# Fewer rows in the small experts' gathers and scatters, and another row order for the down weights and the activation

## The reference

```
gu = xb @ w_gate_up[e] + b_gate_up[e]          # 1024 -> 2048, rows xb = tokens of expert e
gate, up = jnp.split(gu, 2, axis=-1)
gate = jnp.minimum(gate, SWIGLU_LIMIT)
up = jnp.clip(up, -SWIGLU_LIMIT, SWIGLU_LIMIT)
act = (up + 1.0) * gate * jax.nn.sigmoid(SWIGLU_ALPHA * gate)
return act @ w_down[e] + b_down[e]             # 1024 -> 1024
...
out = jnp.zeros((n_tok, d)).at[row_token].add(y_rows * row_weight)
```

## Time and profile before

| | us |
|---|---|
| median of 3 runs | 1781.4 |
| lowest and highest run | 1780.25, 1784.91 |
| the profiled execution, its own time | 1781.47 |
| its span | 1779.8 |
| PE busy | 1724.3 |
| DVE busy | 1384.3 |
| ACT busy | 1187.3 |
| POOL busy | 659.3 |
| loads of gate_up chunks, issue to landing (median) | 8.8 |
| loads of down chunks, issue to landing (median) | 10.0 |

### The profile page before, as it was taken

The page is one execution under the profiler, slowest core; times in us unless marked ns, Lnnn a source line. Parts: engine busy times, 40 slices in busy tenths (PEclk is TensorE's granted clock), DMA queues, the critical chain, the costliest instruction groups (busy, mean ns, idle before and its releaser), DMA issues.

```text
span 1779.8 us, 25410 instructions
## 1 busy us (share of the span) xinstructions
PE 1724.3 (97%) x8657; PEld 1393.4 (78%) x8657; DVE 1384.3 (78%) x1048; ACT 1187.3 (67%) x952; POOL 659.3 (37%) x344
## 2 busy tenths in 40 slices
PE   6999999999999999999999999999999999999998
PEld 5888888777888977777777777777777777777776
DVE  4666775754334499999999999999999999999984
ACT  5655555343222377887787787787787887887775
POOL 6224233550000162454454454454454454454110
PEclk9999999999999999999999999999999999999999
DMA  5443434343337379999999999999999999999961
GB/s 177 122 130 84 124 113 113 112 137 88 95 99 273 122 256 384 404 389 389 396 389 387 398 395 387 396 391 388 399 394 389 399 395 387 400 395 388 400 207 48
DMA packets 151821, 504.61 MB, mean 284 GB/s; under 512 B 13692, under 2 KB 74244, under 8 KB 118132
## 3 DMA queue, kind: packets, MB, share of 16 engines
q1 hardware_dynamic: 141652, 478.49, 70.1%
q0 software_dynamic: 10064, 25.28, 5.9%
q10 hardware_dynamic: 48, 0.07, 0.0%
HBM read 489.60 MB, written 22.25 MB: 288 GB/s over the span
## 4 chain that ended last, share of the span: by engine, by line
PE 72%; DVE 10%; issue 8%; ACT 6%; POOL 2%; DMA 1%; ACTq 0%; DVEq 0%; POOLq 0%
PE gu_ps L2356 13%; PE dn_ps L2400 11%; PE gu_ps L2108 8%; PE gu_ps L2110 8%; PE gu_ps L2109 8%; PE gu_ps L2360 7%; DVE split_l L1891 6%; PE dn_ps L2406 6%; PE et_ps L2342 2%; ACT split_h L1286 2%; ACT fold L1298 2%; PE dn_ps L2592 1%; PE gu_ps L2592 1%; PE gu_ps L2130 1%; PE gu_ps L2370 1%
## 5 line engine op out<-in xcount | busy, mean ns | idle before, releaser
L1891 DVE TENSOR_TENSOR split_l<-ring,split_h 128x2048 fp32r<-128x2048 f32 x384 | 867.7, 2286 | 82.4 <-ACT split_h L1286 81.5
L1286 ACT ACTIVATE split_h<-ring 128x2048 fp32r<-128x2048 f32 x384 | 730.1, 1913 | 146.5 <-PE gu_ps L2360 62.7
L910 POOL COPY icur<-slots 96x1 int32 x30 | 197.5, 6582 | 464.8 <-PE et_ps L2342 462.6
L1499 DVE TENSOR_TENSOR w_lo<-w_raw,w_hi 128x2048 fp32r<-128x2048 f32 (+1 forms) x45 | 104.0, 2312 | 129.6 <-ACT w_hi L1018 123.8
L2400 PE MATMUL dn_ps<-split_h,actT_h 128*128 128x512 f32 x496 | 159.2, 402 | 0.0
L2108 PE MATMUL gu_ps<-hT_h,w_hi 128*128 128x512 f32 x392 | 154.4, 394 | 0.6 <-DVE acc L1552 0.6
L2400 PE MATMUL dn_ps<-split_h,actT_l 128*128 128x512 f32 x496 | 154.0, 392 | 0.0
L2110 PE MATMUL gu_ps<-hT_h,w_lo 128*128 128x512 f32 x392 | 152.7, 390 | 0.0
L2109 PE MATMUL gu_ps<-hT_l,w_hi 128*128 128x512 f32 x392 | 152.6, 389 | 0.0
L2370 PE MATMUL gu_ps<-split_l,xgT_h 128*128 128x512 f32 x480 | 136.6, 406 | 14.5 <-DVE split_l L1891 10.7
L2356 PE MATMUL gu_ps<-split_h,xgT_h 128*128 128x512 f32 x512 | 140.6, 396 | 1.0 <-DVE xgT_l L1897 1.0
(11 more groups left out here) (415 smaller groups left out, 3157.5 us busy)
## 6 DMA issues: line engine op xcount, KB each, us to landing
ring<-in_w_gate_up SPq DMA_DIRECT2D x256, 1024.0 KB, 8.8
ring<-in_w_down SPq DMA_DIRECT2D x128, 1024.0 KB, 10.0
w_raw<-in_w_in SPq DMA_DIRECT2D x28, 1024.0 KB, 5.9
arow<-acum_rows POOLq DMA_DIRECT2D x16, 512.0 KB, 6.5
w_raw<-in_w_ssd_out SPq DMA_DIRECT2D x8, 1024.0 KB, 5.2
w_raw<-in_w_in SPq DMA_DIRECT2D x9, 512.0 KB, 6.0
w_raw<-in_w_mix_out SPq DMA_DIRECT2D x4, 1024.0 KB, 7.8
wpg<-in_w_ple_gate SPq DMA_DIRECT2D x2, 2048.0 KB, 21.1
```

The lines of the kernel that those rows point to most:

```text
L910: g.tensor_copy(icur[:, :], col).then_inc(idx_done, 1)
L1286: a.activation(split_h[s % SPLIT][:, :], ring[s % RING][:, :], ACT.Copy).then_inc(hi_done, 1)
L1499: v.tensor_tensor(w_lo[RAW_SLOT[n]][:, 0:size], w_raw[RAW_SLOT[n]][:, 0:size], w_hi[HI_SLOT[n]][:, 0:size].bitcast(F32), ALU.subtract).the ...
L1891: v.tensor_tensor(split_l[s % SPLIT][:, :], ring[s % RING][:, :], split_h[s % SPLIT][:, :].bitcast(F32), ALU.subtract).then_inc(lo_done, 1)
```

## The change

Three edits. (1) POOL's `fetch`, `gather` and `scatter` get a number of rows; in the pass with ranked experts the small ones (positions 2 to 30) are gathered and scattered with 64 rows, the others with 96. The loop of 29 turns becomes one turn ahead and 14 turns of two experts each. (2) The rows of w_down that a partition holds are no longer k*128+p but 8*p+k: a down chunk takes two neighbouring rows of 4 KB per partition. (3) So that block k of the transposed activation holds columns 8*p+k, DVE writes `act_sb` in that order: it reads `silu_sb` and `up_sb` in their order and steps 128 values (512 bytes) with each value written.

```diff
-                src = w_down[0, bass.ds(of, 1), 2 * r * P:(2 * r + 2) * P, :].rearrange("o (k p) f -> (o p) k f", p=P)
+                src = w_down[0, bass.ds(of, 1), :, :].rearrange("o (p k) f -> (o p) k f", k=KD)[:, 2 * r:2 * r + 2, :]
...
-            def fetch():
+            def fetch(rows=ROWS):
...
-                g.indirect_dma_start(out=xg[:, :], out_offset=None, in_=h_rows,
-                                     in_offset=bass.IndirectOffsetOnAxis(ap=icur[:, 0:1], axis=0),
+                g.indirect_dma_start(out=xg[0:rows, :], out_offset=None, in_=h_rows,
+                                     in_offset=bass.IndirectOffsetOnAxis(ap=icur[0:rows, 0:1], axis=0),
...
-                g.indirect_dma_start(out=x1_rows, out_offset=bass.IndirectOffsetOnAxis(ap=dcur[:, 0:1], axis=0),
-                                     in_=y_sb[:, :], in_offset=None, bounds_check=SEQ - 1,
+                g.indirect_dma_start(out=x1_rows, out_offset=bass.IndirectOffsetOnAxis(ap=dcur[0:rows, 0:1], axis=0),
+                                     in_=y_sb[0:rows, :], in_offset=None, bounds_check=SEQ - 1,
...
+                if isinstance(j, int):
+                    rows_of(0, ROWS, ROWS)
+                    with pool.Fori(0, PAIRS - 1) as i:
+                        rows_of(i * 2 + 1, HALF, ROWS)
+                        rows_of(i * 2 + 2, ROWS, HALF)
...
-                v.scalar_tensor_tensor(act_sb[0:rows, :], silu_sb[0:rows, :], SILU_TOP, up_sb[0:rows, :], ALU.min, ALU.mult
-                                       ).then_inc(act_done, 1)
+                natural = lambda m: m[0:rows, :].rearrange("m (p k) -> m p k", k=KD)
+                v.scalar_tensor_tensor(act_sb[0:rows, :].rearrange("m (k p) -> m p k", k=KD), natural(silu_sb),
+                                       SILU_TOP, natural(up_sb), ALU.min, ALU.mult).then_inc(act_done, 1)
```

More of the change, by code:

```diff
@@ L896, in _, with gather @@
                         o.then_inc(win_sum, 1)
-            def fetch():
-                g.indirect_dma_start(out=xg[:, :], out_offset=None, in_=h_rows,
-                                     in_offset=bass.IndirectOffsetOnAxis(ap=icur[:, 0:1], axis=0),
+            def fetch(rows=ROWS):
+                g.indirect_dma_start(out=xg[0:rows, :], out_offset=None, in_=h_rows,
+                                     in_offset=bass.IndirectOffsetOnAxis(ap=icur[0:rows, 0:1], axis=0),
                                      bounds_check=SEQ - 1, oob_is_err=False
                                      ).then_inc(xg_loaded, 16)
-            def gather(m, col, steps):
+            def gather(m, col, steps, rows=ROWS):
                 pool.wait_ge(xg_loaded, 16 * m - 16)
@@ L912, in gather @@
                 alone(pool)
-                fetch()
+                fetch(rows)
             def send(c):
@@ L925, in weigh, with scatter @@
                 g.tensor_copy(wcur[:, :], col).then_inc(w_ready, 1)
-            def scatter(n, col, steps, following=None, landed=True):
+            def scatter(n, col, steps, following=None, landed=True, rows=ROWS):
                 pool.wait_ge(y_evac, n + 2)
@@ L968, in one_pass @@
                 pool.wait_ge(et_done, t0 + 2)
-                gather(m0 + 2, slots[0:ROWS, column(2), 0], k0 + 3)
+                small = HALF if isinstance(j, int) else ROWS
+                gather(m0 + 2, slots[0:ROWS, column(2), 0], k0 + 3, small)
                 if isinstance(j, int):
@@ L972, in one_pass, with rows_of @@
                     pool.sem_inc(y_free, 1)
-                with pool.Fori(0, NE - 3) as e:
+                def rows_of(e, rows_in, rows_out):
                     pool.wait_ge(et_done, t0 + e * 2 + 4)
-                    gather(m0 + e + 3, slots[0:ROWS, column(e + 3), 0], k0 + e * 2 + 4)
-                    scatter(j * NE + e, slots[0:ROWS, column(e), 0], k0 + e * 2 + 5, slots[0:ROWS, column(e + 1), 1].bitcast(F32))
+                    gather(m0 + e + 3, slots[0:ROWS, column(e + 3), 0], k0 + e * 2 + 4, rows_in)
+                    scatter(j * NE + e, slots[0:ROWS, column(e), 0], k0 + e * 2 + 5,
+                            slots[0:ROWS, column(e + 1), 1].bitcast(F32), True, rows_out)
+                if isinstance(j, int):
[3 more added lines that the diff above has]
+                        rows_of(i * 2 + 2, ROWS, HALF)
+                else:
+                    with pool.Fori(0, NE - 3) as e:
+                        rows_of(e, ROWS, ROWS)
                 for e in range(NE - 3, NE - 1):
                     scatter(j * NE + e, slots[0:ROWS, column(e), 0], k0 + NE + e + 1, slots[0:ROWS, column(e + 1), 1].bitcast(F32),
-                            not isinstance(j, int) or e < NE - 2)
+                            not isinstance(j, int) or e < NE - 2, small if e == NE - 2 else ROWS)
                 if not isinstance(j, int):
```

## The result

The changed kernel takes 1772.88 us (median; 1772.75 to 1773.93), the kernel before 1781.4 (median of five runs, 1780.25 to 1784.91). The ratio is 0.9948 with a 95% interval of 0.9936 to 0.9959. So the change makes the kernel faster by half a per cent; forecast were 1784.2 us and a range of 1776 to 1798, and both are wrong.

A forecast was written before the change was run, and what follows sets the result against it. PE and the DMA engines were both taken as near their end. Product 0.75 us later, fold 0.1 sooner, less 0.47 slack: 0.18 us a turn, 2.7 us over 15 turns on 1781.47, so 1784.2 us, range 1776 to 1798.

The forecast's parts named there:

- The term of the 64 rows: Small expert's scatter ahead of the fold: a third fewer rows brings the fold 0.2 us sooner a turn, bounds 0 and 0.2.
- The term of the late buffers: Half stage's last four gate_up loads issue 0.75 us later as DVE frees buffers later; the fold comes 0.2 us later.
- All that any relief can give back: PE's idle time in the expert loop, 1.4 us a turn, 21 us over 15 turns, 1.2%.
- The product: DVE's write of act_sb with a step: 0.75 us more, 1.97 us instead of 1.22.
- PE's new wait: Half stage, down chunk 3: product's 0.75 us more less 0.47 slack makes PE wait 0.28 us; 0.18 with the sooner fold.
- POOL is hidden: POOL issues gathers some 33 us ahead of their reader, so its longer program costs nothing unless many us late.
- The packets: Down loads in 8 KB packets: 0.05 us less a load; the two ahead of the fold land 0.1 us sooner.
- in a stretch where no engine waits for a load: Small expert's gather at 1005.5 to 1008.5: 64 rows save up to 0.14 us there, counted as no gain.
- The relief outweighs: Rival: stepped write nearly free, loads in time, the fold's wait of at most 7.6 us goes; 1773.9 us, chance 0.08.
- Late buffers in full: Rival: late loads carried fully to the fold, 0.45 us later; 0.73 us a turn, 1792.4 us, chance 0.17.
- a product of 1.5 us more: Rival: the stepped write costs 1.5 us more, PE loses 1.76 us a turn; 1808 us, chance 0.13.
- slow down loads: Rival: down loads in pieces 32 KB apart take twice 2.45 us, 19.6 us a turn more; 2075 us, chance 0.03.

The follow-up runs named there:

- experiment 1: Kernel before with only the 64-row transfers for small experts, down weights and product as before: 1773.65 us.
- experiment 4: Kernel before with only the stepped product, loads and 96 rows as before: 1778.91 us.
- experiment 9: Kernel before (96 rows, plain product) with one added POOL wait that issues the large gather at -12.8 instead of -20.3: 1779.94 us.
- experiment 10: Kernel before with 64-row transfers and an added POOL wait that issues the large gather at -12.8; 4 KB packets, plain product: 1772.25 us.
- experiment 2: Kernel before with the 8 KB down packets and the stepped product, all row transfers of 96: 1778.35 us.
- 11: Changed kernel with the product written in order as before, 64 rows and 8 KB packets kept: 1773.58 us.
- 12: Changed kernel with down weights read as before in 4 KB packets, 64 rows and stepped product kept: 1773.75 us.

## Why the prediction was wrong

Two steps failed. The term of the 64 rows, 0.2 us of a sooner fold in a turn, was mis-sized: 0.88 was measured, and this alone brings the whole gain (experiment 1, 1773.65 us). The term of the late buffers, 0.2 us of a later fold, had the wrong sign: the stepped product alone brings the fold 1.05 us sooner (experiment 4).

**What bounds the kernel: half right.** "All that any relief can give back" was put at 21 us, and at the join 7.6 us. The measured gain, 8.4 us of span, is the wait for the fold, 7.6, and 0.8 elsewhere. The floor of 66.19 us a turn is 0.57 below the turn of before, near the 0.5 that the row of the fold gave. What I didn't see is that PE's wait for the fold was most likely the loads' pace itself: with 96 rows the loads fall behind PE from turn to turn (by 0.46 and 0.22 us in experiment 9) and four kernels settle at 66.62 to 66.76 us a turn, with 64 they keep up with PE (experiment 10). By this reading, which is argued from the row of turns, the wait was no matter of two late loads, but the place at which the pace of all 24 came to PE. I had both shares, PE at 195.7 of 200 and DMA at 1.01, in the earlier trace rows and took the second as background.

**(1) The product: right, off by 0.1.** 2.07 us was measured for 1.97; the addition is 0.85, not 0.75. Some luck is in it: the two reductions of the earlier trace rows differ not by the step alone, but also in what they write (32 values in bf16 against 4 in f32). The Vector Engine (DVE) Microarchitecture Reference of the Trainium skill (Measured stream behaviour on trn2) led to 0.67 or 1.48; the trace's 0.85 / 1024 = 0.83 ns more for a value lies nearer to its hop of 4 KB than to its step of 24 words. PE's new wait, forecast at 0.28 a turn, is 0.85 - 0.47 = 0.38 by the same sum, and experiment 4 has 5.8 / 15 = 0.39 on the weight loads. In the changed kernel it is nearly gone, since the fold and with it the chain to down chunk 3 come earlier. In the full stage DVE's two pauses swallow the product and the waits at the half gate_up stay 10.7 us, as forecast.

**The late buffers: the step that failed by its sign.** The loads are issued later, as I said (0.77 for the first four of the half stage, 0.43 for down chunk 0, 0 for chunk 1), but the down chunks come 1.0 us sooner in experiment 4, not 0.2 later. What I left out is that POOL runs beside DVE. POOL's copy takes 1.3 us in all kernels with the plain product that start it at -22.5, and 9.3 in all with the stepped one. With the copy the large gather moves from -20.3 to -12.3 and the small scatter from -12.7 to -6.9, so that its data moves at -0.8 to +1.3 instead of -6.1 to -3.6. "POOL is hidden" was true of POOL's own time and false of its transfers: I asked whether a later gather would come too late for its reader, not which loads it would meet. That the shift as such brings it is shown by experiment 9, which has it without the step, with ring loads issued as before, the same short first turns, and the same time as near as the runs tell (1779.94 and 1778.91). What it brings is a lead, though, not a faster loop: experiment 2 is back at 66.75 from the sixth turn on. DVE's two missing pauses are not what holds the copy: in the kernel before it has ended at 1024.4, five us ahead of the first of them (1029.58), and in the changed kernel it ends at 1029.85, where DVE has no pause. What the product changes is where in a split the copy starts, 0.2 us instead of 1.0 behind its beginning; why it is then not released with that split stays open. The page SBUF — State Buffer of the Trainium skill (Two separate sides) has it that a GpSimd instruction that reads SBUF is locked out for the whole of a VectorE instruction with two SBUF inputs that started first. The trace agrees in that both copies end where a split ends, to 0.1 us, but the rule alone gives 2 us and not 9.3: the long copy also goes past the end of its first split and past the operation at 1022.52, which reads PE's sums and one tile.

**(2) The packets: right, as far as these runs can tell.** I gave 0.1 us a turn, 1.5 us in all, which is about the spread of the runs; experiment 2 against 4, 11 against 1 and 12 against the changed kernel show no difference beyond that. That a pitch of 32 KB does no harm was right, too. Only pieces of 4 KB that lie 16 KB apart, which the change doesn't have, cost 4.4 us.

**(3) The 64 rows: the mis-sized term.** I allowed 0.2 us a turn for the small scatter, a third of 0.63, and nothing for the small gather. Measured: 64 rows alone bring the fold 0.88 us forward (+1.83 to +0.95) and turns 6 to 14 down by 0.51; the scatter alone makes 0.46 of it and the gather alone 0.15 (one execution of each kernel). Two errors lie in it. First, "a third of the rows gone can save up to a third" was taken of the wrong time. The small scatter's packets did lose a third, but of their own 2.84 us, which is 0.9, and not of the 0.63 that the loads lost in rate. The rows that are gone moved no bytes, while those that remain are dealt out anew over the DMA engines. The trace doesn't name the engine of a packet, so what follows is argued, not shown: with equal shares on 16 engines 96 rows are 6 each and 64 rows 4, so two row packets of 4 KB fewer on the engine that is last, at 0.26 us each in the trace 0.52 us for each transfer by an estimate, more where the load's own packets stand between them, and a load that is spread over all engines ends with the last. What speaks for it: in each of the four pairs that differ by the 64 rows alone (before and 1, 2 and after, 4 and 12, 9 and 10) the small scatter's packets take 0.67 to 0.71 of their time with 96, nearly the 4 to 6 of this account. What speaks against it: the small gather's take 0.77 to 0.93. By DMA: Bandwidth & Descriptors of the Trainium skill (Why a DMA increments its semaphore by 16 and not by 1) a transfer of 96 or 64 partitions is dealt over all 16 engines, which no run here shows. Second, "in a stretch where no engine waits for a load" doesn't make a transfer free when the loads run at their pace all turn long.

**The rivals.** "The relief outweighs" gave 1773.9 us and is what came, within 1.0 us, but by other reasons than I gave: the write was not nearly free, and it was the rows that relieved. I held 0.3 us of sooner landing against it where 0.9 to 1.3 came, and gave it 0.08. Late buffers in full, a product of 1.5 us more and slow down loads did not come.

**What stays open.** Whether rows are dealt out as I argued above; no run here varied the number of rows further. Why the copy is held past the end of its split. And the pace of the loads with 96 rows is known only roughly: turns 6 to 14 take 66.62 in experiment 4 and 66.75 in experiment 2, and the last four of experiment 9 point to 66.4. I don't know whether the product's later ring loads have a part in experiment 4's; experiment 9 shows only that the same gain comes without them.

## What to carry to other kernels

When PE and the DMA engines both run near their end, a short wait for a load can be the pace of all loads, and then every transfer counts, also those for which nobody waits: look at the lengths of the turns one by one, since a loop that starts short and then settles higher has used up a lead. Then look for a single long turn and at the clock beside it before taking a mean for a pace. A change on one engine can move the transfers that another issues: before calling an engine hidden, list what it will issue later and which loads that will meet. Indirect transfers should be cut to the rows that can be valid, not padded with indices that are skipped.

## What the runs showed of the hardware that I had not expected

- A GpSimd copy of 96 values took 1.3 us where it started 1.0 us into a VectorE split (two inputs, 2.29 us), 9.3 us where it started 0.2 us into the same split, and 12.7 us in the full stage of the kernel before; each time it ended where a split ended, not where VectorE paused.
- A VectorE product of 1024 values in a row that writes with a step of 512 bytes took 2.07 us, in order 1.22.
- A float32 transpose on PE whose stationary operand is read with a step of 8 values took 204 ns for the weight load and 274 for the matmul, in order 141 and 246.
- Cutting an indirect scatter from 96 to 64 indices, with the same valid rows, shortened its stretch of packets from 2.84 to 1.96 us beside 1 MB loads; with two such transfers in each of 15 turns the kernel went from 1779.94 to 1772.25 us (experiments 9 and 10).
- In one execution the granted clock fell to 0.50 for some three microseconds twice, each time 1 to 2 us behind a wait of PE (2.09 and 1.64 us). The turn with the first took 3.7 us more than PE's 66.2.
